# Two of the eight one-hot rows of each pick-weight group made on GpSimd instead of VectorE

## The chip, the core and the metric

The kernel runs on one core of a Trainium2 chip. The metric is the device time of one execution in microseconds (us). The kernel before takes 1502.49 us, the median of three runs (1501.68 to 1503.31).

## The reference, cut to what matters

The kernel computes two layers one after the other. The first ends in PEER, a layer with 16384 single-neuron experts, of which every token picks 8 heads x 16; the place of the change is in PEER.

```python
def peer_ffn(xn, w_q, sub_keys, u, v):
    ...
        s = jnp.einsum('thpd,hpnd->thpn', q, sub_keys).astype(jnp.float32)
        s_top, i_top = lax.top_k(s, PEER_TOPK)
        cand = s_top[:, :, 0, :, None] + s_top[:, :, 1, None, :]
        ...
        best, pos = lax.top_k(cand, PEER_TOPK)
        expert = jnp.take_along_axis(cand_idx, pos, axis=-1)
        g = jax.nn.softmax(best, axis=-1)
        act = jax.nn.gelu(jnp.einsum('td,thkd->thk', xb, u[expert]), approximate=False)
        return jnp.einsum('thk,thkd->td', (g * act).astype(xb.dtype), v[expert])
```

An expert's number is (first key) x 128 + (second key). There are 256 tokens, so 256 x 128 picks, each with two keys and a weight g.

## The kernel before, in words

The kernel gathers no experts. It builds for every token a dense 128 x 128 matrix G of pick weights (first key by second key), then walks over all 128 second keys, computes the activations of the 128 experts that share it, multiplies by the slice of G and adds the products with their rows of v. The walk (u_pass and v_pass on TensorE) is the long middle of the execution.

**The build of G.** The picks of a token stand in `chosenT` with the 128 slots as partitions: row 0 the first key, row 1 the second key, row 2 the weight. Two one-hot matrices per token are made from it, 128 slots x 128 keys each: `hotA` (1 where the slot's first key equals the column) and `hotB` (the slot's weight where its second key equals the column). TensorE multiplies them into the token's G in PSUM. Tokens go in NG = 32 groups of GRP = 8; `hotA` and `hotB` have GBUF = 2 buffers, each for one group. Both, `chosenT` and `dist` lie in the space of `ring` and are named so in the profile; `iota` and `act_j` are named `oi`, G is named `big`.

Each engine's program is written out by hand and runs in order; engines meet only at semaphores:

- VectorE (`onehots`): waits until TensorE has done the group that used the buffer (`g_mm`), makes all eight `hotA` matrices in one TENSOR_TENSOR (L1510), then seven `hotB` rows, k = 1 to 7, each one TENSOR_SCALAR with two per-partition scalars (L1513). It raises `onehot_ready` after k = 3 and after k = 7: two halves of four tokens.
- ScalarE (`distances`, `hot_row`): row k = 0 of each group in two activations (L1002, L1008). It also copies every finished half of a group from PSUM to G (L992, `g_evac`, raises `g_out`).
- TensorE: for each half waits for `onehot_ready` (first halves also for ScalarE's row) and for a free PSUM bank (`g_out`), does four products (L2097; two records each), raises `g_mm`, and then one piece of `ahead` (L2075), a chunk of the u_pass of one of the first eight second keys. The chunks run out after half 57 of 64.
- GpSimd has nothing to do in the build. Its last work before it is sums of the picks (L758 to L763), its next a memset after the walk (L767).

After the last group VectorE splits one tile (`split_lo_early(0)`, L1540), TensorE goes on to its first u_pass (L2107 to L2111) and, once `g_out` has reached 64, the walk begins. SP's queue loads the first rows of v when TensorE has done keys 7 and 8 of `ahead`, and one row of u when `g_mm` is at 64.

Of the kernel before, what the change touches and what calls it, by code (L numbers as in the profile page):

```python
# [9 lines left out]
ALU = mybir.AluOpType  # L10
# [18 lines left out]
LEVELS = 7  # L29
# [10 lines left out]
GT = 4  # L40
GRP = 2 * GT
GBUF = 2
ROUNDS = 4


FULL = 4
CAND = FULL * TOP + (TOP - FULL) * 4
NG = T // GRP
# [55 lines left out]
def build(nc, t, out):  # L104
    ctx = ExitStack()
    with ctx:
# [3 lines left out]
        def sem(name):  # L110
            return ctx.enter_context(nc.semaphore(name))
# [8 lines left out]
        ident = sb("ident", [P, P])  # L120
        oi = sb("oi", [P, 2, P])
        ones, iota = oi[:, 0], oi[:, 1]
        act_j = oi[:].rearrange("p a b -> p (a b)")
        upper = sb("upper", [P, P])
        masks = sb("masks", [P, LEVELS + 1, P], U8)
# [111 lines left out]
        cum_done = sem("cum_done")  # L237
        lb_in_then_sum = sem("lb_in_then_sum")
        lb_exp_then_rest_out = sem("lb_exp_then_rest_out")
        masks_done = sem("masks_done")  # L240
        lvl_exponent = sem("lvl_exponent")
        lvl_decay = sem("lvl_decay")
        lvl_scaled = sem("lvl_scaled")
# [16 lines left out]
        pickT_done = sem("pickT_done")  # L260
# [5 lines left out]
        g_mm = sem("g_mm")  # L266
# [105 lines left out]
        chosenT = takeR(3, T)  # L372
        hotA = takeR(GBUF, GRP, NKEY)
        takeR = arena(ring[:, 2, D:], KC * TILE - D)
        hotB = takeR(GBUF, GRP, NKEY)
# [322 lines left out]
        def _(pool):  # L698
# [55 lines left out]
            for r in range(ROUNDS - 1):  # L754
                for a in range(2):
                    pool.wait_ge(matched, 2 * r + a + 1)
                    kept = pick[:, r % 2, a]
                    link(pool.tensor_tensor(kept, kept, round_keys(r, a), ALU.mult))  # L758
                    for m in (8, 4, 2):
                        link(pool.tensor_tensor(kept[:, :, :, 0:m], kept[:, :, :, 0:m], kept[:, :, :, m:2 * m], ALU.add))  # L760
                    for n in range(NT):
                        dst = chosen[:, n, a].rearrange("p (h k) -> p h k", h=PH)[:, 2 * r:2 * r + 2]
                        ins = pool.tensor_tensor(dst, kept[:, 2 * n:2 * n + 2, :, 0], kept[:, 2 * n:2 * n + 2, :, 1], ALU.add)  # L763
                    ins.then_inc(pick_kept, 1)

            pool.wait_ge(wl_done, NKEY)
            pool.memset(ones, 1.0).then_inc(consts_made, 1)  # L767

            for n in range(NT):
                f, x, half = slice(n, n + 1), slice(n, n + 1), mhalf[:, 0:1]  # L770
# [482 lines left out]
        def _(dve):  # L1253
# [71 lines left out]
                mark(dve.tensor_scalar(ge[:, l], xf, float(1 << l), None, ALU.is_ge))  # L1325
            wait_marked()
            dve.tensor_tensor(masks[:, 0:LEVELS], ge[:, 0:LEVELS], ge[:, 1:LEVELS + 1], ALU.subtract)
            dve.tensor_copy(masks[:, LEVELS], ident[:]).then_inc(masks_done, 1)
            piece_split_lo("hf0")
            dve.wait_ge(lb_exp_then_rest_out, 1)  # L1330
            link(dve.tensor_tensor(lbs, lbe[:, 0], lbe[:, 1], ALU.add))
# [34 lines left out]
            for l in range(LEVELS + 1):  # L1366
                m = 1 << l
                b = l % 2
                dve.wait_ge(lvl_decay, l + 1)
                if l >= 2:  # L1370
                    dve.wait_ge(lvl_scores, 2 * l)
                half = lambda a: a.rearrange("p f (b two m) -> p (f b) two m", two=2, m=m)
                dve.tensor_tensor(half(qd[:, b])[:, :, 1, :], half(qF)[:, :, 1, :], half(dec[:, b])[:, :, 1, :], ALU.mult)
                dve.tensor_tensor(half(kd[:, b])[:, :, 0, :], half(kF)[:, :, 0, :], half(dec[:, b])[:, :, 0, :], ALU.mult).then_inc(lvl_scaled, 1)
                if l == 0:
                    dve.wait_ge(masks_done, 1)
                    piece_split_lo("hgate1")
                keep(l, masks[:, LEVELS if l == 0 else l - 1])
                if 1 <= l <= 4:
                    piece_split_lo(next_piece(LEVEL_PIECES1[l - 1], 2))  # L1380

            dve.wait_ge(group_out, group_no["ggate1"] + 1)
            for n in range(NT):
                for a in range(2):
                    g = gate1[:, n, a * TILE:(a + 1) * TILE].rearrange("p (h v) -> p h v", h=4)
# [12 lines left out]
            for k in range(4):  # L1398
                half, n = k // 2, k % 2
# [105 lines left out]
            def onehots(g):  # L1505

                buf, tok = g % GBUF, slice(g * GRP, (g + 1) * GRP)
                if g >= GBUF:
                    dve.wait_ge(g_mm, 2 * (g - GBUF) + 2)
                dve.tensor_tensor(hotA[:, buf], bcast(iota, 1, GRP), bcast(chosenT[:, 0, tok], 2, NKEY), ALU.is_equal)  # L1510
                for k in range(1, GRP):
                    at = slice(g * GRP + k, g * GRP + k + 1)
                    ins = dve.tensor_scalar(hotB[:, buf, k], iota, chosenT[:, 1, at], chosenT[:, 2, at], ALU.is_equal, ALU.mult)  # L1513
                    if k % GT == GT - 1:
                        ins.then_inc(onehot_ready, 1)

            for g in range(NG):
# [77 lines left out]
            for k, name in enumerate(("dnq", "dnk", "dnv")):  # L1595
                dve.wait_ge(g2_out, g2_no[name + "1"] + 1)
                for tap in reversed(range(CONV)):
                    for f in range(4 * k, 4 * k + 4):
# [6 lines left out]
                        else:  # L1605
                            ins = dve.scalar_tensor_tensor(convT[:, f], src, w, convT[:, f], ALU.mult, ALU.add)
# [225 lines left out]
        def _(pe):  # L1832
# [256 lines left out]
            for g in range(NG):  # L2089
                pe.wait_ge(onehot_by_act, g + 1)  # L2090
                for half in range(2):
                    n = 2 * g + half
                    pe.wait_ge(onehot_ready, n + 1)
                    if n >= 4:
                        pe.wait_ge(g_out, n - 3)
                    for k in range(GT):
                        ins = pe.matmul(ps[:, n % 4, k * P:(k + 1) * P], hotA[:, g % GBUF, half * GT + k], hotB[:, g % GBUF, half * GT + k], start=True, stop=True)  # L2097
                    ins.then_inc(g_mm, 1)
                    ahead(CHUNKS_BEFORE_BUILD + n, CHUNKS_BEFORE_BUILD + n + 1)
# [375 lines left out]
```

## Time and profile before

| | |
|---|---|
| median of three runs | 1502.49 us |
| the profiled execution's own time | 1502.27 us |
| its span in the trace | 1500.5 us |
| mean granted TensorE clock | 0.982 |
| TensorE matmul busy | 1421.7 us (95%) |
| VectorE busy | 1011.2 us (67%) |
| ScalarE busy | 734.0 us (49%) |
| GpSimd busy | 93.2 us (6%), 104 instructions |

The table is of the whole span; the change is in a stretch of about 95 us of it, from 293 to 389 us. Busy shares of the whole span say little of that stretch. A record of an instruction lasts from its start to its last write, and on VectorE the next record starts before the last one has ended, so the step from one start to the next is shorter than the duration.

### The profile page before, as it was taken

What the parts mean: (1) busy time and instruction counts of PE and PEld (TensorE: products, weight loads), DVE (VectorE), ACT (ScalarE), POOL (GpSimd) and SP (SyncE); (2) the same over time, 40 slices, a digit from 0 to 9 for tenths busy, and PEclk for the clock granted to TensorE, in tenths of its full rate; (3) what the DMA queues carried; (4) which work ended last, traced back from release to release, by engine and by line L of the source; (5) the groups of instructions that cost most, each with busy time, mean ns of one, the idle gap of its engine ahead of it and who ended that gap; (6) DMA issues with size and microseconds to landing.
All of it is one profiled execution on the core that took longest, in us unless ns stands there. A gap on an engine that the chain in (4) does not pass through costs nothing.

```text
span 1500.5 us, 21930 instructions
## 1 busy us (share of the span) xinstructions
PE 1421.7 (95%) x7790; PEld 1217.0 (81%) x7790; DVE 1011.2 (67%) x1814; ACT 734.0 (49%) x1108; POOL 93.2 (6%) x104
## 2 busy tenths in 40 slices
PE   6998899899999999999999999999889999998996
PEld 6877688588788888888888888888788899887885
DVE  6577458999766666666666666666665565655664
ACT  4644312276555555555555555555446633364333
POOL 0052124300000000000000000000010100000000
PEclk9999899999999999999999999999988999999999
DMA  5532262111365555555555555555533332433432
GB/s 178 189 129 73 102 221 99 42 57 43 128 197 191 186 193 185 192 184 194 185 191 186 193 186 191 185 193 186 183 138 140 141 113 85 148 133 142 171 136 98
DMA packets 56006, 229.13 MB, mean 153 GB/s; under 512 B 6656, under 2 KB 6928, under 8 KB 47120
## 3 DMA queue, kind: packets, MB, share of 16 engines
q1 hardware_dynamic: 55488, 228.19, 44.3%
q8 instruction: 36, 0.59, 0.2%
q10 hardware_dynamic: 464, 0.20, 0.0%
q14 instruction: 18, 0.15, 0.0%
HBM read 226.27 MB, written 2.10 MB: 152 GB/s over the span
## 4 chain that ended last, share of the span: by engine, by line
PE 84%; DVE 8%; ACT 4%; DMA 1%; issue 1%; POOL 0%; ACTq 0%; POOLq 0%; DVEq 0%
PE ps L2122 22%; PE ps L1945 13%; PE ps L2111 13%; PE ps L1912 9%; PE ps L2109 7%; PE ps L2097 4%; PE ps L1869 3%; PE ps L2075 2%; PE ps L2107 2%; DVE lo L1314 2%; ACT hi L847 1%; PE ps L1985 1%; PE ps L2225 1%; PE ps L2235 1%; DMA raw<-in_pieces 1%
## 5 line engine op out<-in xcount | busy, mean ns | idle before, releaser
L1523 DVE TENSOR_TENSOR lo<-raw,hi 128x1024 fp32r<-128x1024 f32 x238 | 290.8, 1222 | 63.1 <-ACT hi L986 63.1
L2111 PE MATMUL ps<-x,hi 128*128 128x512 f32 x840 | 301.9, 398 | 0.0
L986 ACT ACTIVATE hi<-raw 128x1024 fp32r<-128x1024 f32 x238 | 250.4, 1052 | 0.0
L2109 PE MATMUL ps<-x,lo 128*128 128x256 f32 x960 | 249.7, 281 | 0.0
L1945 PE MATMUL ps<-hi,x 128*128 128x512 f32 x704 | 229.2, 401 | 2.8 <-DVE lo L1314 2.3
L1314 DVE TENSOR_TENSOR lo<-raw,hi 128x2048 fp32r<-128x2048 f32 x62 | 143.0, 2308 | 90.7 <-ACT hi L847 90.7
L2109 PEld LDWEIGHTS ps<-x,lo 128*128 128x128 f32 x960 | 181.6, 189 | 9.3
L2111 PEld LDWEIGHTS ps<-x,hi 128*128 128x128 f32 x840 | 157.8, 188 | 33.7
L1945 PEld LDWEIGHTS ps<-hi,x 128*128 128x128 f32 x704 | 135.2, 192 | 33.7 <-DVE lo L1314 2.7
L1029 ACT ACTIVATE oi<-ps 128x256 f32<-128x256 f32 x120 | 46.0, 383 | 234.6 <-PE ps L2111 233.4
L2122 PE MATMUL ps<-hi,wh 128*128 128x512 f32 x500 | 155.7, 392 | 3.5 <-DVE wl L1533 2.6
L847 ACT ACTIVATE hi<-raw 128x2048 fp32r<-128x2048 f32 x62 | 118.4, 1910 | 81.4 <-PE ps L1945 48.3
L2122 PE MATMUL ps<-lo,wh 128*128 128x512 f32 x500 | 155.2, 392 | 0.0
L2122 PE MATMUL ps<-hi,wl 128*128 128x512 f32 x500 | 153.9, 389 | 0.0
L1945 PE MATMUL ps<-lo,x 128*128 128x512 f32 x352 | 139.3, 396 | 0.0
L1528 DVE TENSOR_TENSOR oi<-oi,ps 128x256 f32<-128x256 f32 x120 | 50.5, 421 | 96.0 <-ACT oi L1029 96.0
L2122 PEld LDWEIGHTS ps<-hi,wl 128*128 128x128 f32 x500 | 93.9, 188 | 20.8
L2122 PEld LDWEIGHTS ps<-lo,wh 128*128 128x128 f32 x500 | 93.9, 188 | 20.8
L2122 PEld LDWEIGHTS ps<-hi,wh 128*128 128x128 f32 x500 | 93.4, 188 | 20.6 <-issue 3.3
L1912 PE MATMUL ps<-x,hi 128*128 128x256 f32 x544 | 101.8, 290 | 3.4 <-DVE x L1298 2.5
L1533 DVE TENSOR_TENSOR wl<-oi,wh 128x256 fp32r<-128x256 f32 x120 | 51.0, 425 | 59.4 <-ACT wh L1038 59.4
L1912 PEld LDWEIGHTS ps<-x,hi 128*128 128x128 f32 x544 | 87.3, 197 | 4.3 <-DVE lo L1314 3.7
(372 smaller groups left out, 2081.5 us busy)
## 6 DMA issues: line engine op xcount, KB each, us to landing
raw<-in_v_t SPq DMA_DIRECT2D x128, 512.0 KB, 3.5
raw<-in_u_t SPq DMA_DIRECT2D x126, 512.0 KB, 3.5
raw<-in_pieces SPq DMA_DIRECT2D x62, 1024.0 KB, 4.8
ring<-in_peer_w_q SPq DMA_DIRECT2D x4, 2048.0 KB, 9.6
big<-in_up SPq DMA_DIRECT2D x4, 2048.0 KB, 9.3
ring<-in_w_mem_kv SPq DMA_DIRECT2D x2, 2048.0 KB, 8.4
resid<-in_x SPq DMA_DIRECT2D x1, 1024.0 KB, 5.4
big<-in_mem SPq DMA_DIRECT2D x1, 1024.0 KB, 5.1
```

What stands on the lines that cost most here:

```text
L847: act.activation(part_of(hi2, name), raw_piece(name), ACT.Copy).then_inc(piece_hi, 1)
L986: act.activation(hi[:, which, par], raw[:, which, par], ACT.Copy).then_inc(hi_done[which], 1)
L1314: dve.tensor_tensor(part_of(lo2, name), raw_piece(name), part_of(hi2, name).bitcast(F32), ALU.subtract).then_inc(piece_lo, 1)
L1523: dve.tensor_tensor(lo[:, which, par], raw[:, which, par], hi[:, which, par].bitcast(F32), ALU.subtract).then_inc(lo_done[which], 1)
L1528: dve.tensor_tensor(act_j, act_j, ps[:, par, 0:T], ALU.add).then_inc(lb_in_then_sum, 1)
L1533: dve.tensor_tensor(wl[:], act_j, wh[:].bitcast(F32), ALU.subtract).then_inc(wl_done, 1)
L1912: ins = pe.matmul(o, a, b, start=(c == 0 and k == 0), stop=(c == chunks - 1 and k == 2))
L1945: ins = pe.matmul(o, a, b[:, c], start=(s == 0 and c == 0 and k == 0), stop=(s == 1 and c == HALF - 1 and k == 2))
L2097: ins = pe.matmul(ps[:, n % 4, k * P:(k + 1) * P], hotA[:, g % GBUF, half * GT + k], hotB[:, g % GBUF, half * GT + k], start=True, stop=True)
L2109: pe.matmul(first, u_lo[:, par, c], xh[:, c], start=False, stop=False)
L2111: ins = pe.matmul(both, u_hi[:, par, c], x2[:, :, c], start=False, stop=(c == KC - 1))
L2122: ins = pe.matmul(ps[:, 4 + 2 * tau + half, :], w[:, tok], v[:, V, par, half * TILE:(half + 1) * TILE], start=(first and k == 0), stop=(la ...
```

## The change

In every group GpSimd makes the `hotB` rows k = 6 and 7, with the same operation; VectorE makes k = 1 to 5; ScalarE keeps k = 0. GpSimd waits for `chosenT` (`pickT_done`) and, from the third group on, for the same `g_mm` value as VectorE. It counts its groups on the semaphore that was `masks_done` (renamed; its first count is the old one), and TensorE waits for it before each second half. VectorE raises `onehot_ready` after k = 3 and k = 5.

```diff
+POOL_ROWS = 2
...
+            pool.wait_ge(pickT_done, 2)
+            for g in range(NG):
+                if g >= GBUF:
+                    pool.wait_ge(g_mm, 2 * (g - GBUF) + 2)
+                for k in range(GRP - POOL_ROWS, GRP):
+                    at = slice(g * GRP + k, g * GRP + k + 1)
+                    ins = pool.tensor_scalar(hotB[:, g % GBUF, k], iota, chosenT[:, 1, at], chosenT[:, 2, at], ALU.is_equal, ALU.mult)
+                ins.then_inc(masks_then_pool_rows_done, 1)
+
             pool.wait_ge(wl_done, NKEY)
...
-                for k in range(1, GRP):
+                for k in range(1, GRP - POOL_ROWS):
                     at = slice(g * GRP + k, g * GRP + k + 1)
                     ins = dve.tensor_scalar(hotB[:, buf, k], iota, chosenT[:, 1, at], chosenT[:, 2, at], ALU.is_equal, ALU.mult)
-                    if k % GT == GT - 1:
+                    if k in (GT - 1, GRP - POOL_ROWS - 1):
                         ins.then_inc(onehot_ready, 1)
...
                     pe.wait_ge(onehot_ready, n + 1)
+                    if half:
+                        pe.wait_ge(masks_then_pool_rows_done, g + 2)
```

On VectorE the first three groups stood so before (L1501 scales the weights for ScalarE; `ring` here is `chosenT`, `hotA` and `hotB`):

```order
279 L1501 TENSOR_SCALAR ring<-ring 128x256 [waits pickT_done]
280 L1510 TENSOR_TENSOR ring<-oi,ring 128x1024 [waits pickT_done]
281 L1513 TENSOR_SCALAR ring<-oi,ring 128x128 x7
282 L1510 TENSOR_TENSOR ring<-oi,ring 128x1024
283 L1513 TENSOR_SCALAR ring<-oi,ring 128x128 x7
284 L1510 TENSOR_TENSOR ring<-oi,ring 128x1024 [waits g_mm]
285 L1513 TENSOR_SCALAR ring<-oi,ring 128x128 x7
```

and stand so now:

```order
279 L1511 TENSOR_SCALAR ring<-ring 128x256 [waits pickT_done]
280 L1520 TENSOR_TENSOR ring<-oi,ring 128x1024 [waits pickT_done]
281 L1523 TENSOR_SCALAR ring<-oi,ring 128x128 x5
282 L1520 TENSOR_TENSOR ring<-oi,ring 128x1024
283 L1523 TENSOR_SCALAR ring<-oi,ring 128x128 x5
284 L1520 TENSOR_TENSOR ring<-oi,ring 128x1024 [waits g_mm]
285 L1523 TENSOR_SCALAR ring<-oi,ring 128x128 x5
```

Each group has lost two rows there, and nothing else of VectorE's program has moved.

On GpSimd the last sums of the picks and the memset after the walk followed each other before:

```order
78 L760 TENSOR_TENSOR big<-big 128x64x2 [waits pool_step]
79 L763 TENSOR_TENSOR big<-big 128x32 [waits pool_step]
80 L763 TENSOR_TENSOR big<-big 128x32
81 L767 MEMSET oi 128x128 [waits wl_done]
82 L708 TENSOR_SCALAR small<-small 128x1 [waits sumsq_done]
```

Now the rows stand between them (L773; the first four are two groups, since both buffers are free at first; the pattern of two rows goes on to the 32nd group):

```order
80 L764 TENSOR_TENSOR big<-big 128x32
81 L773 TENSOR_SCALAR ring<-oi,ring 128x128 [waits pickT_done]
82 L773 TENSOR_SCALAR ring<-oi,ring 128x128 x3
83 L773 TENSOR_SCALAR ring<-oi,ring 128x128 [waits g_mm]
84 L773 TENSOR_SCALAR ring<-oi,ring 128x128
85 L773 TENSOR_SCALAR ring<-oi,ring 128x128 [waits g_mm]
86 L773 TENSOR_SCALAR ring<-oi,ring 128x128
```

So GpSimd gets 64 instructions, and a wait at the first of each pair.

## Rows read from the trace of the kernel before

**Rows 1.** Windows: busy time of each engine in two stretches, granted clock (PEclk), DMA.

```profile
core 0: us, PE busy (x) PEld busy (x) DVE busy (x) ACT busy (x) POOL busy (x), PEclk, DMA share, GB/s
...
302.90:381.00 78.10, 77.00 (x536) 65.79 (x535) 78.10 (x215) 52.24 (x117) 0.00 (x0) 1.00 0.13 42
...
400.00:1080.00 680.00, 677.26 (x3398) 571.27 (x3396) 457.17 (x611) 365.50 (x608) 0.00 (x0) 1.00 0.57 188
```

**Rows 2.** Groups by line, 290 to 395 us: busy us, mean ns, idle before.

```profile
L1513 DVE TENSOR_SCALAR ring<-oi,ring 128x128 f32<-128x128 f32 x224 | 60.1, 340 | 0.0
...
L1510 DVE TENSOR_TENSOR ring<-oi,ring 128x1024 f32<-128x1024 f32 x32 | 39.0, 1217 | 0.0
L992 ACT ACTIVATE big<-ps 128x512 f32<-128x512 f32 x64 | 38.1, 597 | 30.1 <-PE ps L2097 29.9
```

**Rows 3.** Timeline, first groups of the build: start us, duration us, engine, line.

```profile
293.46 1.23 DVE L1510 TENSOR_TENSOR ring<-oi,ring 128x1024 f32<-128x1024 f32 x1
...
296.23 1.08 PEld L2097 LDWEIGHTS ps<-ring 128*128 128x128 f32 x8
...
302.85 1.08 PEld L2097 LDWEIGHTS ps<-ring 128*128 128x128 f32 x8
```

**Rows 4.** Timeline, one group in the steady part.

```profile
308.12 1.21 DVE L1510 TENSOR_TENSOR ring<-oi,ring 128x1024 f32<-128x1024 f32 x1
...
308.46 1.08 PEld L2097 LDWEIGHTS ps<-ring 128*128 128x128 f32 x8
...
309.26 1.88 DVE L1513 TENSOR_SCALAR ring<-oi,ring 128x128 f32<-128x128 f32 x7
...
310.18 0.97 PEld L2097 LDWEIGHTS ps<-ring 128*128 128x128 f32 x8 [0.41 <-issue]
...
311.05 1.22 DVE L1510 TENSOR_TENSOR ring<-oi,ring 128x1024 f32<-128x1024 f32 x1
```

**Rows 5.** Timeline, the last group and what follows it.

```profile
384.31 1.22 DVE L1510 TENSOR_TENSOR ring<-oi,ring 128x1024 f32<-128x1024 f32 x1
...
386.38 1.98 PEld L2097 LDWEIGHTS ps<-ring 128*128 128x128 f32 x16 [0.95 <-issue]
...
387.24 1.22 DVE L1540 TENSOR_TENSOR lo<-ring,hi 128x1024 fp32r<-128x1024 f32 x1
...
388.58 0.19 PEld L2107 LDWEIGHTS ps<-x,hi 128*128 128x128 f32 x1 [0.23 <-issue]
```

**Rows 6.** Groups by line of GpSimd, whole span, shapes apart.

```profile
L760 POOL TENSOR_TENSOR big<-big 128x128 f32<-128x128 f32 x6 | 2.5, 411 | 0.5
...
L708 POOL TENSOR_SCALAR small<-small 128x8 f32<-128x8 f32 x2 | 0.4, 202 | 18.4 <-DVE small L1389 18.4
...
L773 POOL TENSOR_TENSOR small<-small 128x1 f32<-128x1 f32 x2 | 0.4, 194 | 0.2
...
L716 POOL TENSOR_SCALAR_AFFINE_SELECT ident<-ident 128x128 f32<-128x128 f32 x1 | 0.3, 292 | 0.2 <-POOL mhalf L713 0.2
```

**Rows 7.** Timeline, 72 to 83 us, VectorE and GpSimd (same shape at 75.05 and 79.22).

```profile
75.05 2.26 DVE L1314 TENSOR_TENSOR lo<-raw,hi 128x2048 fp32r<-128x2048 f32 x1
...
78.60 1.47 POOL L738 TENSOR_TENSOR big<-big 128x768 f32<-128x768 f32 x1
79.22 2.99 DVE L1314 TENSOR_TENSOR lo<-raw,hi 128x2048 fp32r<-128x2048 f32 x1 [1.91 <-ACT hi L847]
```

**Rows 8.** Timeline, 1086 to 1094 us, VectorE and GpSimd.

```profile
1089.54 0.55 POOL L709 TENSOR_TENSOR small<-small,mhalf 128x1 f32<-128x1 f32 x1
...
1090.47 0.75 DVE L1584 TENSOR_SCALAR big<-big,small 128x1024 f32<-128x1024 f32 x1 [1.34 <-POOL small L777]
1090.72 0.91 POOL L709 TENSOR_TENSOR small<-small,mhalf 128x1 f32<-128x1 f32 x1
```

**Rows 9.** One line's instructions, whole span: duration ns min/median/max.

```profile
L1445 DVE TENSOR_TENSOR big<-big x8: 350/404/551, 211.0 to 274.8; 128x256 f32<-128x256 f32 x4, 128x192 f32<-128x192 f32 x4
```

**Rows 10.** Timeline, 273 to 276 us (128x256, then 128x128 on GpSimd; 128x256, then 128x192 on VectorE).

```profile
273.84 1.27 POOL L760 TENSOR_TENSOR big<-big 128x256 f32<-128x256 f32 x2
...
274.45 0.87 DVE L1445 TENSOR_TENSOR big<-big 128x256 f32<-128x256 f32 x2
```

More of the change, by code:

```diff
@@ L239, in build @@
         lb_exp_then_rest_out = sem("lb_exp_then_rest_out")
-        masks_done = sem("masks_done")
+        masks_then_pool_rows_done = sem("masks_then_pool_rows_done")
         lvl_exponent = sem("lvl_exponent")
@@ L1327, in _ @@
             dve.tensor_tensor(masks[:, 0:LEVELS], ge[:, 0:LEVELS], ge[:, 1:LEVELS + 1], ALU.subtract)
-            dve.tensor_copy(masks[:, LEVELS], ident[:]).then_inc(masks_done, 1)
+            dve.tensor_copy(masks[:, LEVELS], ident[:]).then_inc(masks_then_pool_rows_done, 1)
             piece_split_lo("hf0")
@@ L1375, in _ @@
                 if l == 0:
-                    dve.wait_ge(masks_done, 1)
+                    dve.wait_ge(masks_then_pool_rows_done, 1)
                     piece_split_lo("hgate1")
```

## The prediction

> **What bounds the kernel now.** I read the page's shares first: TensorE is busy for 95% of the span, GpSimd for 6%. That says nothing of the stretch of the change, so I took the windows of it. From 302.9 to 381 us VectorE is busy for all of its 78.10 us, TensorE (whose ends are modelled) for 77.00, ScalarE for 52.24, GpSimd for nothing, at a granted clock of 1.00 [rows 1]. The groups by line then show that VectorE's two lines have no idle time before them, while ScalarE's copies spend 29.9 us waiting for TensorE [rows 2]. The timeline shows who paces whom. A group starts on VectorE at 308.12 and the next at 311.05, 2.93 us apart, and TensorE's first half at 310.18 has stood idle 0.41 us ahead of it [rows 4]; the weight loads before it are not released by another engine in the trace ("issue"), but the fourth row of `hotB` is done just then: 309.26 plus three steps and a duration, below. The period holds from the first group to the last: 293.46 to 384.31 is 31 periods of 2.931 us [rows 3, 5]. TensorE alone would be faster: while it still had stock, five halves took 302.85 - 296.23 = 6.62 us, 1.324 each, so 2.65 us a group [rows 3]. So VectorE is the bound of the build by 0.28 us a group, and TensorE is next.
>
> What follows the build is TensorE's: 677.26 of 680 us busy in the walk [rows 1]. Its first u_pass starts at 388.58, when the last products end (386.38 + 1.98 = 388.36) and VectorE's split of 387.24 ends (388.46) [rows 5]. The loads and copies of the walk's start are released by counts of this same work, so they move with it, and I take every us of the build as a us of the whole.
>
> **What is removed.** 64 TENSOR_SCALAR on VectorE, two a group. The step of one, from start to start, is (1.88 - 0.34)/6 = 0.257 us [rows 2, 4]. TENSOR_TENSOR's step is 309.26 - 308.12 = 1.14, and 1.14 + 7 x 0.257 = 2.94 gives the period back. Without two rows VectorE would need 2.93 - 0.514 = 2.42 us a group, less than TensorE's 2.65.
>
> **What is added.** Two TENSOR_SCALAR of 128x128 on GpSimd a group, which has not run that shape. Nearest from below is AFFINE_SELECT, one source of the same size, 0.292; nearest from above TENSOR_TENSOR, two sources, 0.411 [rows 6]. TENSOR_SCALAR itself has 0.202 at 8 columns, against 0.194 for the other operation at one; on so short a stretch it does not grow more slowly than by 1 ns a column, which gives 0.32 at 128. Two operations with two per-partition scalars stand nearer to the upper row for me: I take d = 0.37, and keep 0.29 to 0.41 as the bounds from rows and 0.5 as what a slow operation would be. Two rows take some 0.7 of 2.65 us, so GpSimd by itself is no bound. Its order after `g_mm` leaves it time too: it wakes when TensorE ends group g, with its rows wanted in the second half of g + 2, almost two groups later.
>
> **What the two engines do to each other.** This decides the case. GpSimd's TENSOR_TENSOR of 78.60 to 80.07 overlapped a VectorE TENSOR_TENSOR from 79.22; that took 2.99 instead of 2.26: VectorE stood until 0.12 before the other's end [rows 7]. The other way round, VectorE's TENSOR_SCALAR of 1090.47 to 1091.22 held a GpSimd instruction that takes 0.55 alone until 1091.63 (0.91): after VectorE's end it needed 0.41, so 0.14 of its work had been done in waiting [rows 8]. Both operations of the build on VectorE are of these two kinds, so they exclude GpSimd's rows and are excluded by them. What one GpSimd instruction costs a busy VectorE is seen once: at 274.45 two VectorE instructions follow each other and a 0.411 instruction of GpSimd gets in between them [rows 6, 10]; the second takes 0.551 instead of 0.350 [rows 9]. The price is 0.20, not 0.41: the start of each is worked off while the other runs, and VectorE's records overlap by 0.34 - 0.257 = 0.08 anyway [rows 2, 4]. So I price a GpSimd row at D = d - 0.21, which is 0.16 for d = 0.37 (0.08 for 0.29, 0.20 for 0.41).
>
> The Trainium skill has a stricter rule in SBUF — State Buffer, Who interferes with whom: VectorE with two SBUF inputs, or a tensor_scalar in a two-port mode, and GpSimd share one pair of ports as a lock, and "the other fully blocks" for a whole instruction. That they exclude each other the trace bears out; taken as a full duration, the rule would charge VectorE with 0.37 a row.
>
> **The other edits.** TensorE's extra wait stands before second halves. First halves have two or three waits already and ran at 1.324 a half all the same [rows 3], so a satisfied wait costs nothing; if it does cost, 32 x 0.05 = 1.6 us is my upper bound. Behind it in TensorE's queue is everything, but it is late only if GpSimd's rows are, for which the slack above would have to go. The counts on `onehot_ready` after k = 5 come earlier than k = 7 did. ScalarE has 52.24 of 78.10 us of work in 26.6 groups, 1.96 a group, below 2.65 [rows 1]; its copies come every 1.32 instead of 1.47 us and take 0.597 [rows 2].
>
> **The sum.** VectorE's new period is 2.416 + 2 x 0.16 = 2.74 us, above TensorE's 2.65, so VectorE still paces. Over 31 periods: 31 x (2.93 - 2.74) = 5.9 us less. The profiled execution's own time is 1502.27 (span 1500.5), which gives 1496.4; the median of the runs stands 0.22 higher, so the forecast for the runs is 1496.6. In short: each moved row saves VectorE 0.257 and costs it D.
>
> **Rivals.**
>
> *TensorE takes over* (D below 0.117, d below 0.33). Then a group costs 2.65 and 31 x 0.28 = 8.7 us go; 1493.8. For it: the one-source row of 0.292 [rows 6]. The last three groups have no chunks of `ahead` and take VectorE's time, which eats at most 0.5 of this. Against it: two operations and two scalars. The Trainium skill would say the same: GPSIMD Engine Reference, Elementwise — side-by-side cycle accounting, has the body of at most two operations at 1.03 cycles an element; an estimate from it is 128 x 1.03/1.2 = 110 ns above the 0.194 of one column, 0.30. No row here shows this for TENSOR_SCALAR.
>
> *Saving and cost cancel* (D between 0.21 and 0.305, d 0.42 to 0.515): within 3 us of before. For it: GpSimd's TENSOR_TENSOR is at 0.411 already and the new operation has more operands.
>
> *A row costs more than it saves* (the other sign, from D = 0.257, by over 0.2% from D = 0.305). Mechanism: VectorE is held for the whole of GpSimd's row, as the lock read strictly has it. With D = 0.37 the period is 2.42 + 0.74 = 3.16 and the kernel takes 31 x 0.23 = 7.1 us longer, 1509.6; a d of 0.58 under my own rule does the same. Against it: the pair of rows at 274.45, where half of the instruction was hidden [rows 9, 10]; but there both were TENSOR_TENSOR, and there is one such case.
>
> *GpSimd doesn't get in* while VectorE's instructions follow each other, and makes its rows only when VectorE waits for `g_mm`. Then TensorE's second half is late by both rows: some 2.42 + 0.7 + 0.1 = 3.2 a group, 31 x 0.27 = 8.4 us longer, 1510.9. Against it: at 274.45 it got in at the first boundary [rows 10].
>
> **How the numbers follow.** Chances: the forecast (d 0.33 to 0.42) 0.39, TensorE takes over 0.25, cancel 0.17, a row costs more 0.13, GpSimd kept out 0.06. A measurement of this kernel can tell about 0.2%, 3.0 us, from no change. Faster is the first two, 0.64; same 0.17; slower 0.19. The range goes from TensorE's bound with a little for the tail and the runs' scatter, 1493.3, to 1503.5, which takes in most of the case of cancelling and leaves out the two slow cases.
>
> **What would show it.** Right: on VectorE five rows in the timeline between L1520s 2.65 to 2.8 us apart; single TENSOR_SCALAR of VectorE lengthened by 0.1 to 0.2 where a GpSimd row stands beside them, two a group; GpSimd's rows at 0.3 to 0.6 in the records, waits included; TensorE's first products of the last group some 6 us earlier than 386.38, and the walk of the same length. TensorE the bound: VectorE shows idle time released by TensorE before L1520. Wrong: periods of 2.9 or more, VectorE's rows lengthened by 0.26 or more, GpSimd's rows over 0.5 where VectorE stands still, or TensorE idle before second halves with GpSimd as releaser.

## The result and the profile after

The changed kernel takes 1491.78 us (median of four runs, 1491.56 to 1492.91) against 1502.28 us before (four runs, 1501.68 to 1503.31): ratio 0.993, 95% interval 0.9918 to 0.9943. Its profiled execution has a span of 1489.8 us. It is faster, as forecast, but by 10.5 us where 5.7 were forecast (1502.28 - 1496.6), and below the range.

The windows of the changed kernel, over the steady part of the build and its end (columns as in [rows 1]):

```profile
303.00:372.00 69.00, 69.00 (x523) 66.30 (x522) 66.70 (x158) 50.48 (x111) 69.00 (x53) 1.00 0.14 47
372.00:379.50 7.50, 6.55 (x53) 5.98 (x52) 6.49 (x14) 7.13 (x13) 5.62 (x5) 1.00 0.19 70
```

TensorE and VectorE have changed places against [rows 1]: TensorE is busy throughout, VectorE has 2.30 us idle in 69. GpSimd, idle there before, is busy for all of it, which 64 rows of 0.37 could not have done. The groups by line:

```profile
L773 POOL TENSOR_SCALAR ring<-oi,ring 128x128 f32<-128x128 f32 x64 | 84.3, 1329 | 18.3 <-DVE ring L1509 17.5 <-PE ps L2109 0.8
...
L1523 DVE TENSOR_SCALAR ring<-oi,ring 128x128 f32<-128x128 f32 x160 | 45.3, 363 | 0.0
L1520 DVE TENSOR_TENSOR ring<-oi,ring 128x1024 f32<-128x1024 f32 x32 | 39.3, 1228 | 2.7 <-PE ps L2109 0.2
```

A GpSimd row has 1.329 us in the records, three and a half times my 0.37. VectorE's rows went from 340 to 363 ns [rows 2]. The timeline of two groups, VectorE and TensorE:

```profile
303.42 1.22 DVE L1520 TENSOR_TENSOR ring<-oi,ring 128x1024 f32<-128x1024 f32 x1
303.44 1.08 PEld L2109 LDWEIGHTS ps<-ring 128*128 128x128 f32 x8
...
304.56 1.42 DVE L1523 TENSOR_SCALAR ring<-oi,ring 128x128 f32<-128x128 f32 x5
...
304.76 1.08 PEld L2109 LDWEIGHTS ps<-ring 128*128 128x128 f32 x8
...
306.06 1.22 DVE L1520 TENSOR_TENSOR ring<-oi,ring 128x1024 f32<-128x1024 f32 x1
306.08 1.08 PEld L2109 LDWEIGHTS ps<-ring 128*128 128x128 f32 x8
```

The idle 0.41 us ahead of TensorE's first halves [rows 4] are gone. A group takes 306.06 - 303.42 = 2.64 us, TensorE's rate of [rows 3]. VectorE's five rows take 1.42; five at the old step would be 4 x 0.257 + 0.34 = 1.37. So both GpSimd rows cost it 0.05 together, and after them it stands for 0.08 (304.56 + 1.42 to 306.06) until TensorE's products of the group that used the buffer are done: the sign that the prediction named for TensorE as the bound, though the profile names TensorE as releaser for only 0.2 of the 2.7 us. GpSimd's own timeline of the same stretch, from two narrow windows:

```profile
303.59 1.81 POOL L773 TENSOR_SCALAR ring<-oi,ring 128x128 f32<-128x128 f32 x1
```

```profile
305.38 0.87 POOL L773 TENSOR_SCALAR ring<-oi,ring 128x128 f32<-128x128 f32 x1
```

The row that meets VectorE's TENSOR_TENSOR takes 1.81, the one beside its TENSOR_SCALARs 0.87. The first group is different:

```profile
292.58 0.90 POOL L773 TENSOR_SCALAR ring<-oi,ring 128x128 f32<-128x128 f32 x1 [17.52 <-DVE ring L1509]
```

```profile
292.83 1.35 DVE L1520 TENSOR_TENSOR ring<-oi,ring 128x1024 f32<-128x1024 f32 x1
```

Here the row had started 0.25 us before the TENSOR_TENSOR and was not held, and VectorE's instruction took 1.35 instead of 1.22. All eight profiles in which GpSimd makes rows show this, once each.

To find where the 10.5 us went I split each span at two points that every profile has: VectorE's first TENSOR_TENSOR of the build, and GpSimd's memset behind the walk. Before, from 293.5 to 1080.6, 787.1 us; after, from 292.8 to 1071.5, 778.7. So build and walk give 8.4 us, and it is the build's: from the end of the last product to the memset it takes 692.1 us before and 692.2 after. What lies behind the memset went from 419.9 to 418.3 us, and the stretch ahead of the build is 0.6 us shorter.

### The profile page after: what moved, and what is told of

It reads as the page before. It is cut to its first block, busy times and chain, and to the rows that moved or that the text cites. A ratio compares the mean times of both kernels' runs of the same rounds, so it can differ in the third digit from the quotient of the medians.

```text
span 1489.8 us, 21932 instructions
## 1 busy us (share of the span) xinstructions
PE 1412.4 (95%) x7790; PEld 1216.5 (82%) x7790; DVE 999.4 (67%) x1750; ACT 733.7 (49%) x1108; POOL 177.4 (12%) x168
## 4 chain that ended last, share of the span: by engine, by line
PE 84%; DVE 9%; ACT 4%; DMA 1%; issue 1%; POOL 0%; ACTq 0%; POOLq 0%; DVEq 0%
PE ps L2134 22%; PE ps L1955 13%; PE ps L2123 13%; PE ps L1922 9%; PE ps L2121 8%; PE ps L2109 4%; PE ps L1879 3%; PE ps L2085 2%; PE ps L2119 2%; DVE lo L1324 2%; PE ps L1995 1%; ACT hi L857 1%; PE ps L2237 1%; PE ps L2247 1%; DMA raw<-in_pieces 1%
```

## The experiments

### The same two kernels again

The changed kernel, timed and profiled once more, and the kernel before, profiled once more.

> The changed kernel as it is, timed once more and profiled on another execution. Between the two first profiles the build of G accounts for 8.46 us of 10.7; 0.63 us lie ahead of it and 1.63 us between the walk and the second layer, where the granted clock differs between the two profiles (0.84 against 0.88 and 0.82 against 0.89 in two windows). If these two pieces are scatter of the clock (my theory), they change from profile to profile and the mean gain is 8.5 to 10.5 us; if they belong to the change (rival: an earlier end of the build changes how loads or the clock fall later), they come back with the same size, 10.5 us.

> The kernel before, profiled once more, to see how far the stretches ahead of the build and behind the walk differ between two executions of the same program. Scatter of the clock: 0.5 to 2 us there, and the build 92.3 us again from VectorE's first to its last group. Rival, they belong to the change: these stretches repeat within 0.2 us.

The changed kernel: 1491.65 us (five runs) against 1501.82 (fifteen), ratio 0.9927, interval 0.9914 to 0.9941; span 1490.6. The kernel before: span 1499.4. From the first group to the memset they take 778.8 and 787.1 us: the 8.4 us repeat. Ahead of the build the two repeats take 293.4 and 292.1, the order the other way round, so that piece is scatter. Behind the memset they take 418.4 and 420.2: that piece came back, which I had not expected. The section on the piece behind the walk takes it up. The expectation has 92.3 us from VectorE's first to its last group in the kernel before; it is 90.9 in both profiles.

### What a row costs GpSimd alone

```diff
+            scratch = wh[:, 0:P]
+            pool.wait_ge(consts_made, 1)
+            link(pool.tensor_scalar(scratch, upper[:], mhalf[:, 0:1], mhalf[:, 1:2], ALU.is_equal, ALU.mult))
+            link(pool.tensor_scalar(scratch, upper[:], mhalf[:, 0:1], mhalf[:, 1:2], ALU.is_equal, ALU.mult))
+            link(pool.tensor_scalar(scratch, upper[:], mhalf[:, 0:1], mhalf[:, 1:2], ALU.mult, ALU.add))
+            link(pool.tensor_scalar(scratch, upper[:], mhalf[:, 0:1], None, ALU.mult))
+            link(pool.tensor_scalar(scratch, upper[:], 2.0, 1.0, ALU.mult, ALU.add))
+            link(pool.tensor_tensor(scratch, upper[:], ident[:], ALU.mult))
```

> The kernel before, with six instructions of 128x128 on GpSimd near 3 us, when VectorE does nothing: the row's own operation twice (is_equal and mult with two per-partition scalars, one source), the same with mult and add, with one scalar and one operation, with two constants, and a TENSOR_TENSOR. Their results go nowhere. Theory A (GpSimd's row is long by itself and takes the shared access for a small part of it): the first two take 0.8 to 0.9 us. Theory B (the row is short, as I had it, 0.3 to 0.45 us, and the 0.86 to 1.8 us in the records of the changed kernel are waits for VectorE): 0.3 to 0.45. TENSOR_TENSOR 0.41 in both.

GpSimd's timeline of that kernel, in the order of the diff:

```profile
2.67 0.81 POOL L726 TENSOR_SCALAR wh<-upper,mhalf 128x128 fp32r<-128x128 f32 x1
3.58 0.79 POOL L727 TENSOR_SCALAR wh<-upper,mhalf 128x128 fp32r<-128x128 f32 x1
4.47 0.46 POOL L728 TENSOR_SCALAR wh<-upper,mhalf 128x128 fp32r<-128x128 f32 x1
5.03 0.61 POOL L729 TENSOR_SCALAR wh<-upper,mhalf 128x128 fp32r<-128x128 f32 x1
5.72 0.31 POOL L730 TENSOR_SCALAR wh<-upper 128x128 fp32r<-128x128 f32 x1
6.12 0.46 POOL L731 TENSOR_TENSOR wh<-upper,ident 128x128 fp32r<-128x128 f32 x1
```

The row takes 0.80 us: theory A. VectorE was not idle meanwhile, as the expectation has it, but ran memsets (1.29 to 3.05 and 3.64 to 6.26 us); the contest below has the row once with VectorE idle, at 0.79. The comparison is what costs: with mult and add on the same operands it is 0.46. With mult, add and constants it is 0.31. My two bounds, 0.292 and 0.411 [rows 6], hold for mult and add and missed the operation itself.

### What two more rows cost VectorE

```diff
+        spare = takeR(4, NKEY)
...
+            pool.wait_ge(pickT_done, 2)
+            for g in range(NG):
+                if g >= GBUF:
+                    pool.wait_ge(g_mm, 2 * (g - GBUF) + 2)
+                for k in range(GRP - 2, GRP):
+                    at = slice(g * GRP + k, g * GRP + k + 1)
+                    if spared >= 4:
+                        pool.wait_ge(pool_step, steps[0] - 3)
+                    pool.tensor_scalar(spare[:, spared % 4], iota, chosenT[:, 1, at], chosenT[:, 2, at], ALU.is_equal, ALU.mult).then_inc(pool_step, 1)
```

> The kernel before, with VectorE making all seven rows as ever, and GpSimd making copies of rows 6 and 7 of every group into a spare place, with the same waits; nobody uses them, except that the walk waits once for the last of them. So VectorE saves nothing and pays only GpSimd's price, with TensorE not in the way (2.65 against 2.93 us a group). My prediction's price of 0.16 a row: period 3.25, 10 us longer than before. Theory A, 0.03 a row as the changed kernel's records have it (1.42 instead of 1.37 for five TENSOR_SCALAR): period 3.0, 2 us longer. Theory B, VectorE goes first and GpSimd waits: period 2.93 to 2.95, under 0.7 us longer, and GpSimd's records longer than in the changed kernel.

Measured 1502.91 us against 1501.82, ratio 1.0007, interval 0.9997 to 1.0016. In the profile the first and the last group's TENSOR_TENSOR start at 293.9 and 385.8:

```profile
L1527 DVE TENSOR_TENSOR ring<-oi,ring x32: 1210/1215/1357, 293.9 to 385.8; 128x1024 f32<-128x1024 f32 x32
```

That is 91.9 us for 31 groups against 90.9 before, 1.0 us for 64 GpSimd rows: 0.016 us a row on a VectorE that is never idle, where my prediction had 0.16. The period of 2.96 lies between theories A and B. The price is not even: 21 of the 31 groups take the old 2.93 us and ten take 2.98 to 3.13, the first among them. Where a row costs something, one step of VectorE is 0.05 to 0.13 longer (0.31 to 0.39 instead of 0.257), and the first TENSOR_TENSOR is 0.14 longer. The kernel does nothing useful with the rows, so this is the price by itself.

### The build with the rows for nothing, and with one and three on GpSimd

```diff
-                for k in range(1, GRP):
+                for k in range(1, GRP if g < GBUF else GRP - 2):
...
-                    if k % GT == GT - 1:
+                    if k == GT - 1 or k == (GRP - 1 if g < GBUF else GRP - 3):
```

> The kernel before, with rows 6 and 7 made only in the first two groups (once in each buffer) and left as they are after that; GpSimd makes none. So the weights of two tokens of eight are wrong from the third group on, and the time is that of a build in which two rows cost nothing at all. The price of GpSimd's work in the changed kernel is the difference to it. If TensorE is the bound of the changed kernel (what its trace shows): the same build, 778.8 us from VectorE's first group to the memset after the walk, within 0.3. If GpSimd sets the pace (its records leave no gap, 2.66 us a pair): the build is shorter than that by up to 1 us at the end, where TensorE has no chunks left, and no more, since TensorE needs 2.65 a group. My prediction (VectorE pays 0.16 a row): 2 to 3 us shorter than the changed kernel.

```diff
-POOL_ROWS = 2
+POOL_ROWS = 1
```

> GpSimd makes only row 7, VectorE six. A saved row is 0.257 us on VectorE, and GpSimd's price by the run with two spare rows is 0.02 a row. Then VectorE's period is 2.93 - 0.257 + 0.02 = 2.69, just above TensorE's 2.65: the build 7.4 us shorter than before, 1 us less gained than with two rows. With my prediction's price of 0.16: 2.83, 3 us gained. With the lock for a whole row (0.80 alone, as measured): longer than before.

```diff
-POOL_ROWS = 2
+POOL_ROWS = 3
```

> GpSimd makes rows 5, 6 and 7, VectorE four. A row takes GpSimd 0.80 alone and 0.86 beside VectorE's TENSOR_SCALAR; the one that meets TENSOR_TENSOR took 1.79 with it. If VectorE's two-source instruction holds a GpSimd row up until it ends, three rows need 1.79 + 2 x 0.86 = 3.5 us a group and GpSimd is the bound: 31 x 0.58 = 18 us longer than before. If the 1.79 was only waiting that costs nothing when there is no time (the row would have run elsewhere): 3 x 0.86 = 2.6, TensorE stays the bound, the same time as with two rows.

| kernel | rows on GpSimd | us (before beside it) | ratio, interval | first group to memset |
|---|---|---|---|---|
| before | 0 | 1502.28 | | 787.1 |
| one row | 1 | 1494.38 (1503.12) | 0.9944, 0.9927 to 0.996 | 780.2 |
| changed | 2 | 1491.65 (1501.82) | 0.9927, 0.9914 to 0.9941 | 778.8 |
| two rows dropped | 0 | 1492.01 (1503.12) | 0.9924, 0.9908 to 0.9941 | 778.9 |
| three rows | 3 | 1513.22 (1503.12) | 1.0066, 1.0049 to 1.0083 | 798.1 |

The kernel with dropped rows leaves rows 6 and 7 as they stand from the third group on. Dropping them altogether gains no more than giving them to GpSimd: in the build of the changed kernel GpSimd costs nothing, and TensorE is the bound. In the waits of the kernel with dropped rows, 296 to 380 us, TensorE waits for others once, in the tail:

```profile
ACT big L992 <- PE ps L2097: 20.2, 28, 2.2
PEld ps L2097 <- ACT ring L1008: 1.0, 1, 1.0
```

One row: 6.9 us of the build instead of the 7.4 expected, the first and last group 84.0 us apart (292.0 to 376.0), 2.71 a group where 2.69 was expected, which puts the price of a row at 0.04 here (2.71 - 2.93 + 0.257). VectorE is the bound again, just. Seven of the GpSimd rows there began 0.16 to 0.38 us before a TENSOR_TENSOR and took 1.98 to 2.12 all the same: having started first did not save them. Three rows: the build is 11.0 us longer. I had expected 18, so the place was right and the size was not. The timeline of the kernel with three rows:

```profile
320.78 0.97 PEld L2109 LDWEIGHTS ps<-ring 128*128 128x128 f32 x8 [0.73 <-DVE ring L1523]
...
321.98 1.22 DVE L1520 TENSOR_TENSOR ring<-oi,ring 128x1024 f32<-128x1024 f32 x1 [1.00 <-PE ps L2109]
...
323.12 1.11 DVE L1523 TENSOR_SCALAR ring<-oi,ring 128x128 f32<-128x128 f32 x4
324.03 0.97 PEld L2109 LDWEIGHTS ps<-ring 128*128 128x128 f32 x8 [0.73 <-DVE ring L1523]
...
325.23 1.23 DVE L1520 TENSOR_TENSOR ring<-oi,ring 128x1024 f32<-128x1024 f32 x1 [1.00 <-PE ps L2109]
```

VectorE stands for 1.00 us in every group and TensorE for 0.73; the releaser named for TensorE is a VectorE row, and it is another: narrow windows of GpSimd's timeline have its rows starting at 319.07, 320.70, 321.55, 322.32 and 323.95, without a gap, and TensorE starts 0.08 behind those of 320.70 and 323.95, that is, behind the end of GpSimd's third row. From the third group to the last it does so by 0.07 to 0.08 us. So GpSimd paces at 3.25 us a group: 1.63 + 0.85 + 0.77. Of the three rows only one meets VectorE's TENSOR_TENSOR, and it is held less long than the 1.81 of the changed kernel (1.63); the one that runs while VectorE stands takes 0.77.

### Who holds up whom

Ahead of VectorE's first work, in the kernel before, a contest with known starts. Its core:

```diff
+            six_rows()
+            six_rows()
+            dve.wait_ge(pool_step, 5)
+            link(dve.tensor_tensor(mixed[:, 1], vtok[:, 0], vtok[:, 0], ALU.add))
+            dve.wait_ge(pool_step, 6)
+            long_row()
+            dve.wait_ge(pool_step, 7)
+            long_row()
+            dve.wait_ge(pool_step, 9)
+            six_rows()
```

> The kernel before, with a small contest ahead of VectorE's work at the start of the execution, by itself: six rows on VectorE alone; six rows while GpSimd makes two; a TENSOR_TENSOR of 128x1024 with two SBUF inputs beside one GpSimd row; a TENSOR_SCALAR of 128x1024 with two per-partition scalars beside one row; the same alone; then one GpSimd row and one GpSimd TENSOR_TENSOR alone, and a GpSimd TENSOR_TENSOR beside six rows. Theory A (a GpSimd row takes the shared access in a small part of its 0.80 us): six rows on VectorE take at most 0.1 longer beside two GpSimd rows, the GpSimd row beside TENSOR_TENSOR takes 1.2 + 0.7 us or so, that beside the long TENSOR_SCALAR is held up as well if that reads by two ports (0.8 us long for 1024 columns) and is not if it reads by one (1.2 us long). Theory C (whoever starts first has it for the whole instruction): six rows on VectorE take 0.7 or 1.4 us longer.

VectorE and GpSimd in the timeline of that kernel:

```profile
3.77 3.29 DVE L1299 TENSOR_SCALAR big<-upper,mhalf 128x128 f32<-128x128 f32 x12
5.60 1.96 POOL L728 TENSOR_SCALAR big<-upper,mhalf 128x128 f32<-128x128 f32 x2 [3.05 <-DVE big L1299]
7.67 1.23 DVE L1308 TENSOR_TENSOR big<-big 128x1024 f32<-128x1024 f32 x1 [0.61 <-POOL big L728]
7.74 1.83 POOL L728 TENSOR_SCALAR big<-upper,mhalf 128x128 f32<-128x128 f32 x1 [0.17 <-POOL big L728]
9.67 0.81 DVE L1303 TENSOR_SCALAR big<-big,mhalf 128x1024 f32<-128x1024 f32 x1 [0.77 <-POOL big L728]
9.73 1.33 POOL L728 TENSOR_SCALAR big<-upper,mhalf 128x128 f32<-128x128 f32 x1 [0.17 <-POOL big L728]
11.17 0.81 DVE L1303 TENSOR_SCALAR big<-big,mhalf 128x1024 f32<-128x1024 f32 x1 [0.69 <-POOL big L728]
12.09 0.79 POOL L728 TENSOR_SCALAR big<-upper,mhalf 128x128 f32<-128x128 f32 x1 [1.02 <-DVE big L1303]
...
13.52 1.82 DVE L1299 TENSOR_SCALAR big<-upper,mhalf 128x128 f32<-128x128 f32 x6 [1.54 <-POOL big L732]
```

Twice six rows take 3.29 us, the second six beside two GpSimd rows; at the step of 0.257 twice six take 3.25 plus the hand-over between them. VectorE pays nothing; GpSimd's two rows take 0.98 each instead of 0.79. Beside the TENSOR_TENSOR the GpSimd row takes 1.83 and ends 0.67 after it: it was held by 1.04 us. Beside the long TENSOR_SCALAR it takes 1.33 and was held by 0.54, while VectorE's instruction takes 0.81 with it and without it. So in these pairs VectorE never waits and GpSimd does. The last row is the other case: six rows beside a GpSimd TENSOR_TENSOR take 1.82 instead of 1.63, 0.19 more. That is the price I had read at 274.45 [rows 9, 10], where GpSimd's instruction also had two sources.

The Trainium skill, SBUF — State Buffer, Who interferes with whom, says that of the two the second to start "fully blocks" for a whole instruction. For GpSimd behind VectorE's TENSOR_TENSOR the trace agrees but for 0.12 us (0.67 of the row's 0.79 lie after its end). For VectorE behind a GpSimd TENSOR_SCALAR it does not: 0.00 and on average 0.016 us a row, at most 0.14 (the first TENSOR_TENSOR of the build), against 0.80.

A second contest tried what the price hangs on:

```diff
+            for i in range(4):
+                dve.wait_ge(pool_step, 3 + i)
+                for k in range(5):
+                    row(k)
+                link(row(5))
+            for i in range(4, 6):
+                dve.wait_ge(pool_step, 3 + i)
+                row(0)
+                link(dve.tensor_tensor(mixed[:, 1], vtok[:, 0], vtok[:, 0], ALU.add))
```

> The kernel before, with a second contest ahead of VectorE's work, by itself. Four times six rows on VectorE (1.625 us alone, by the first contest's step) with one other GpSimd instruction of 128x128 started at the same moment: TENSOR_SCALAR mult and add with two per-partition scalars (0.46 alone), is_equal and mult with constants, mult and add with constants (0.31 alone), TENSOR_TENSOR (0.46 alone, 0.20 as its price in the first contest). Then one VectorE row and a TENSOR_TENSOR of 128x1024 behind it, beside the changed kernel's GpSimd row, and the same beside a GpSimd TENSOR_TENSOR. If the price for VectorE follows the number of GpSimd's SBUF sources (two: VectorE stands; one: it doesn't), the first three cost nothing and the fourth 0.2. If it follows how densely the instruction reads (the shorter it is alone for 128 columns, the denser), mult and add with constants costs most, 0.1 to 0.2, and is_equal nothing.

Each set of six rows started when the one before had ended, so the distance of the starts is the measure; 1.67 is the free value (3.77 to 5.44 in the first contest). GpSimd's side:

```profile
3.93 0.61 POOL L727 TENSOR_SCALAR big<-upper,mhalf 128x128 f32<-128x128 f32 x1 [1.38 <-issue]
5.49 0.77 POOL L730 TENSOR_SCALAR big<-upper 128x128 f32<-128x128 f32 x1 [0.94 <-DVE big L1292]
7.23 0.31 POOL L733 TENSOR_SCALAR big<-upper 128x128 f32<-128x128 f32 x1 [0.97 <-DVE big L1292]
8.97 0.45 POOL L736 TENSOR_TENSOR big<-upper,ident 128x128 f32<-128x128 f32 x1 [1.43 <-DVE big L1292]
10.90 1.91 POOL L739 TENSOR_SCALAR big<-upper,mhalf 128x128 f32<-128x128 f32 x1 [1.47 <-DVE big L1292]
11.09 1.22 DVE L1302 TENSOR_TENSOR big<-big 128x1024 f32<-128x1024 f32 x1
```

VectorE's sets start at 3.78, 5.44, 7.18, 8.92 and 10.82: 1.66, 1.74, 1.74 and 1.90. The one-source instructions cost 0.0, 0.07 and 0.07, the two-source one 0.23. The density theory fails: the 0.31 and the 0.77 instruction cost the same. The number of sources explains the large step: the last three all started 0.05 behind VectorE's first row, so at the same distance the second source costs 0.16. The 0.07 where I expected nothing is of the size of the single steps in the kernel with spare rows, and the free instructions started 0.15 behind; what it hangs on stays open. And a VectorE TENSOR_TENSOR that starts 0.19 into a running GpSimd row takes its usual 1.22, while the row takes 1.91. The last pair has a GpSimd TENSOR_TENSOR in place of the row: VectorE's single row ahead of its TENSOR_TENSOR then takes 0.50 from start to start instead of 0.26, 0.24 more.

### The piece behind the walk

Changed kernel, with two or eight memsets of 512 columns between build and walk:

```diff
+        spare = takeR(4, NKEY)
...
+            for _ in range(2):
+                link(dve.memset(spare, 0.0))
             dve.wait_ge(gelu_done, AHEAD)
```

> The changed kernel, with two memsets of 512 columns on VectorE between the build and the walk, about 1.3 us, so that the walk and all behind it start later. Behind the walk the profiles so far have two lengths, 418.1 to 418.4 us (both of the changed kernel, and the one with two rows dropped) and 419.4 to 420.4 (the others), with a dip of the granted clock to 0.89 some 290 us behind the walk in most of the latter. If it hangs on how evenly TensorE is fed in the build, the length stays 418.3. If it hangs on where the end of the walk falls against something that goes on by itself, it can be 419.5 to 420.4 here.

> The same with eight memsets, about 5 us. Same reading: 418.3 behind the walk if the feeding of TensorE in the build decides, another of the lengths seen if the moment does.

Two memsets: the first part is 1.0 us longer (779.7), behind the memset the kernel takes 421.1 us, span 1493.2. Eight: 6.5 us longer (785.3), 418.3 behind, span 1496.7. The window that begins 285 us behind the memset, two memsets first, then eight:

```profile
1357.10:1372.10 15.00, 12.04 (x71) 10.83 (x70) 8.95 (x14) 3.99 (x4) 0.00 (x0) 0.89 0.30 114
```

```profile
1363.40:1378.40 15.00, 11.97 (x68) 10.08 (x67) 7.88 (x9) 4.26 (x5) 0.00 (x0) 1.00 0.48 184
```

In the first TensorE got 0.89 of the full 2.4 GHz on average, in the second all of it, over the same stretch of the program. That is one of two places at which the profiles differ. The other lies some 60 us behind the memset. The kernel before and the changed kernel in their first profiles, from 60 to 75 us behind it:

```profile
1140.60:1155.60 15.00, 15.00 (x57) 12.24 (x58) 5.61 (x10) 11.80 (x12) 0.00 (x0) 0.84 0.19 65
```

```profile
1131.50:1146.50 15.00, 15.00 (x61) 12.22 (x61) 6.38 (x11) 12.24 (x13) 0.00 (x0) 0.91 0.27 88
```

GpSimd's first TENSOR_SCALAR of 128x2 behind the memset parts the two places. Every profile has one of three lengths up to it, within 0.1, and one of two, within 0.2, from it to the end:

| kernel | memset to the 128x2 | from there to the end | sum |
|---|---|---|---|
| changed, both profiles; dropped rows; last kernel below | 102.9 | 315.3 to 315.4 | 418.1 to 418.4 |
| eight memsets | 103.0 | 315.3 | 418.3 |
| three rows; spare rows | 102.9 | 316.6 | 419.5 |
| before, first profile | 104.5 | 315.4 | 419.9 |
| before, second profile; one row; both contests; the six GpSimd instructions | 103.6 to 103.7 | 316.4 to 316.6 | 420.1 to 420.3 |
| two memsets | 104.5 | 316.6 | 421.1 |

So the 1.6 us that the kernel before takes longer there in its first profile lie wholly at the first place, and in its second profile they are 0.8 at the first and 1.1 at the second. Of the 2.8 us of the kernel with two memsets, 1.6 are of the first place and 1.2 of the second. Its build is that of the changed kernel, so the feeding of TensorE in the build alone does not decide; and the moment counted from the start of the program does not either, for the memset stands at 1072.09 with two memsets, at 1072.17 with one row and at 1072.21 in the second profile of the changed kernel, and 421.1, 420.2 and 418.4 us follow. The two delays have one execution each. What decides between these lengths stays open.

### A last row for VectorE

```diff
-                if g + 1 < NG:
+                if g + 1 < NG - 1:
                     hot_row(g + 1)
...
-                for k in range(1, GRP - POOL_ROWS):
+                for k in range(0 if g == NG - 1 else 1, GRP - POOL_ROWS):
```

> The changed kernel, with row 0 of the last group alone made by VectorE instead of ScalarE. In the changed kernel TensorE stands for 0.7 us before the last group, released by ScalarE's row, since ScalarE has a copy of 1.91 us before it, and ScalarE goes on without a gap to its last copies to G, which start the walk. That takes two activations, 0.87 us, out of ScalarE's chain and puts 0.26 on VectorE, which waits there. Expected: TensorE's wait before the last group gone, the walk 0.6 to 0.8 us earlier, 0.05%, which the profile can show and the times hardly can. Rival: ScalarE's other work is the chain and the walk starts at most 0.2 earlier.

1491.10 us against 1502.36, ratio 0.9926, interval 0.9912 to 0.9939: not to be told from the changed kernel by the times. In the profile first group to memset takes 778.4 instead of 778.7 and 778.8. TensorE still waits before the last group, 0.59 instead of 0.73, and now for VectorE's rows. The gain is 0.3 to 0.4 us, between the two theories.

## Why the prediction was wrong

**What bounds the build: right.** VectorE paced it by 0.28 us a group and TensorE was next; the steps, the 2.42 and the 2.65 hold (2.64 measured, and the dropped rows take the same).

**What is added: wrong by a factor of two.** "I take d = 0.37, and keep 0.29 to 0.41 as the bounds from rows and 0.5 as what a slow operation would be". Alone it is 0.80. Both bounding rows were of another operation, and with the comparison the same operands take 0.80 where mult and add take 0.46.

**What the two engines do to each other: the step that failed.** "So I price a GpSimd row at D = d - 0.21". The 0.20 at 274.45 was read rightly and repeats in the contests (0.19, 0.23, 0.24), but it belongs to a GpSimd instruction with two sources, and I carried it to one with one source. In its place VectorE pays 0.016 us a row on average (two spare rows), 0.07 or nothing in the contests. By my own rule the true d of 0.80 would have meant D = 0.59 and a slower kernel, so two errors leaned against each other. That VectorE's instructions exclude GpSimd's was right in one direction: the row waits out the TENSOR_TENSOR, but for the first row of the build. The lengthening of 0.1 to 0.2 that I had named as a sign was 0.05 to 0.07, on two of VectorE's rows a group.

**GpSimd by itself is no bound: right in the outcome, wrong in the working.** I had some 0.7 us for a pair. It takes 2.66 us of records in a period of 2.65, since one of the rows waits out the TENSOR_TENSOR. It ends 1.2 us before it is needed (a pair ends at 306.24, TensorE's second half starts at 307.41), and 0.2 us before in the last group but one, where my slack was almost two groups. The third row shows the limit: 3.25 a group.

**The sum and the rivals.** The forecast of 5.9 us became 8.4 in the build, near the rival "TensorE takes over" (8.7), to which I gave 0.25. I had named its condition rightly, D below 0.117, and tied it wrongly to a d below 0.33. The rivals of the other sign were carried by the same wrong price. The rest, 2 us, comes in the main from behind the walk (1.6 us between the first profiles, 1.8 between the second), where the granted clock falls otherwise; "the walk of the same length" was right, "I take every us of the build as a us of the whole" was not. The range ended at 1493.3 for lack of that: TensorE's bound alone gave 1493.8, within it. That second piece was in no term of the sum, and why it comes is not settled: two executions of the same kernel before lose it at different places, and the delayed kernels show that neither the build nor the moment counted from the start decides it alone.

**The other edits: right.** TensorE's extra wait costs nothing that shows: a half takes 1.32 us as before, and the kernel with dropped rows, which has no such wait, takes the same time. What I had not seen is that TensorE waits 0.73 us for ScalarE's row ahead of the last group, now that VectorE is no longer the later one; 0.3 to 0.4 us of it could be had back.

## What to carry to other kernels

A row of another operation is no bound for the cost on GpSimd: there the same shape took 0.31, 0.46 or 0.80 us by its arithmetic and its scalars alone, so the operation itself is to be measured, as one instruction in an idle moment of a profiled execution. When work goes to GpSimd beside a full VectorE, ask separately what VectorE pays (here nearly nothing for one source, 0.2 us for two) and what GpSimd pays (the length of VectorE's two-source instructions), and count the second against the period, as two rows fitted and three did not. And with a change of 8 us at one place another stage came out 1.6 to 1.8 us shorter, through where the clock's dips fell and for a reason that is not settled, so the stage's own length is the better measure of a change.

## What the runs showed of the hardware that I had not expected

- GpSimd TENSOR_SCALAR of 128x128: 0.31 us (mult, add, constants), 0.46 (the same, two per-partition scalars), 0.61 (one scalar, mult alone), all three beside a VectorE memset; 0.77 beside VectorE's rows (is_equal, mult, constants), 0.79 with VectorE idle (is_equal, mult, two scalars). One operation with one scalar took longer than two with two, in a single instance; mult and add with two scalars took 0.61 too in the second contest, beside VectorE's rows.
- The exclusion between VectorE and GpSimd is nearly one-sided for one-source GpSimd instructions. They are held by 1.04 us beside a TENSOR_TENSOR of 1024 columns and by 0.54 beside a TENSOR_SCALAR of as many columns, which itself takes 0.81 either way. The other way round VectorE lost 0.016 us a row on average, in single steps of 0.05 to 0.13, and 0.14 at the first TENSOR_TENSOR of the build.
- The same stages behind the walk took 418.1 to 421.1 us in 14 profiles, in a few separate lengths, with dips of the granted clock at two places: it was 0.82 to 0.97 in the window from 60 to 75 us behind the memset, and 0.89 or 1.00 in the window from 285 to 300, 0.89 in exactly the eight profiles whose second part is the longer one. Two executions of one kernel differed in which place cost them the time.
